# A projection of fourteen weight blocks by seven products for each pair of blocks

## The reference

```python
h = rmsnorm(x, norm_mix)                                  # 1056 x 1024
proj = h @ w_in                                           # columns q k v z | gates | u v' | c
qkv, new_conv = causal_short_conv(q|k|v, conv_buf, gdn_conv_w)   # 4 taps along tokens, then silu
q, k = l2norm(q), l2norm(k)
o = gated_delta_chunked(q, k, v, g, beta, state)          # o_a
u = gelu(ub); vs = layernorm(gelu(vb)); o_b = u * sgu_mix(vs)
pm = pc + rwkv_mu * (p_prev - pc)                         # then the rwkv7 recurrence, o_c
x = x + concat(o_a, o_b, o_c) @ w_out
x = x + hier_moe(rmsnorm(x, norm_ffn))                    # 16 experts, 2 for each token
y = rmsnorm(x, norm_final)
```

## Time and profile before

| | us |
|---|---|
| median of 3 runs | 1278.34 (1277.28 to 1280.43) |
| the profiled execution | 1276.18 |
| its span | 1274.4 |
| TensorE busy | 1208.9 (95%) |
| VectorE, ScalarE, GpSimd busy | 462.0, 348.8, 523.5 |

### The profile page before, as it was taken

The page is one execution under the profiler, slowest core; times in us unless marked ns, Lnnn a source line. Parts: engine busy times, 40 slices in busy tenths (PEclk is TensorE's granted clock), DMA queues, the critical chain, the costliest instruction groups (busy, mean ns, idle before and its releaser), DMA issues. The chain is left out here.

```text
span 1274.4 us, 31076 instructions
## 1 busy us (share of the span) xinstructions
PE 1208.9 (95%) x12624; PEld 825.0 (65%) x12624; DVE 462.0 (36%) x1140; ACT 348.8 (27%) x821; POOL 523.5 (41%) x790
## 2 busy tenths in 40 slices
PE   9999999999999999999998999959999999999990
PEld 7666666666656668877864554446777777777760
DVE  3135543345375624455441213252222222222223
ACT  4003112533342135555532232211111111111114
POOL 7100000020470036878833021026666666666662
PEclk9999999999999998999999999969999999999995
DMA  6111111125313100010075313279999897999838
GB/s 207 34 34 35 34 33 34 33 50 176 67 33 87 56 17 14 18 23 14 14 228 173 101 67 99 58 278 378 330 373 334 264 371 253 283 371 295 264 50 288
DMA packets 139879, 187.09 MB, mean 147 GB/s; under 512 B 37272, under 2 KB 85903, under 8 KB 139786
## 3 DMA queue, kind: packets, MB, share of 16 engines
q1 hardware_dynamic: 123018, 164.87, 38.3%
q0 software_dynamic: 15936, 20.57, 7.7%
q10 hardware_dynamic: 832, 0.33, 0.1%
HBM read 156.41 MB, written 29.32 MB: 146 GB/s over the span
## 5 line engine op out<-in xcount | busy, mean ns | idle before, releaser
L452 PE MATMUL ps<-hT,w_in 128*128 128x352 f32 (+1 forms) x1296 | 390.7, 461 | 1.8 <-ACT cb L690 1.2
L452 PEld LDWEIGHTS ps<-hT,w_in 128*128 128x128 f32 x1296 | 244.3, 190 | 138.4 <-issue 4.4
L2849 POOL DMA_INDIRECT sum_rows<-slot_out,scatter_rows x76 | 121.6, 1600 | 38.7 <-POOL scatter_rows L2848 25.4
L2894 PE MATMUL ps<-qkv,slot_T 128*32 128x256 f32 x1920 | 109.9, 379 | 2.1 <-DVE slot_T L2981 1.1
L2981 DVE TENSOR_TENSOR slot_T<-slot_raw_T,vecs 128x256 f32<-128x256 f32 x75 | 32.4, 433 | 208.5 <-PE ps L2894 207.6
L2894 PEld LDWEIGHTS ps<-qkv,slot_T 128*32 128x32 f32 x1920 | 74.4, 110 | 31.6 <-DVE slot_T L2981 3.2
L2826 POOL DMA_INDIRECT gathered<-h_rows,gather_rows x79 | 83.4, 1056 | 19.6 <-issue 12.2
L2938 ACT ACTIVATE slot_silu<-ps 128x128 f32<-128x128 f32 x77 | 21.5, 279 | 224.2 <-PE ps L2894 222.0
L2894 PE MATMUL ps<-cb,slot_T 128*32 128x256 f32 x1408 | 80.6, 379 | 0.0
L2894 PEld LDWEIGHTS ps<-cb,slot_T 128*32 128x32 f32 x1408 | 55.2, 110 | 20.8
L2944 ACT ACTIVATE slot_out<-ps,slot_weights 128x256 f32<-128x256 f32 x76 | 36.1, 475 | 112.1 <-PE ps L2905 112.1
(11 more groups left out here) (685 smaller groups left out, 1991.7 us busy)
## 6 DMA issues: line engine op xcount, KB each, us to landing
w_in<-in_w_in SPq DMA_DIRECT2D x28, 512.0 KB, 4.0
qkv<-in_expert_w_gate SPq DMA_DIRECT2D x6, 2048.0 KB
qkv<-in_expert_w_up SPq DMA_DIRECT2D x6, 2048.0 KB
qkv<-in_expert_w_down SPq DMA_DIRECT2D x6, 2048.0 KB
cb<-in_expert_w_gate SPq DMA_DIRECT2D x5, 2048.0 KB
cb<-in_expert_w_up SPq DMA_DIRECT2D x5, 2048.0 KB
zg<-in_expert_w_down SPq DMA_DIRECT2D x5, 2048.0 KB
third_w_down<-in_expert_w_down SPq DMA_DIRECT2D x5, 2048.0 KB
```

The costliest lines, as they stand in the source:

```text
L452: last = pe.matmul(pbank(b)[:, c, 0:n], w[:, k, :], hT[:, k, c * CH:c * CH + n], start=(k == 0), stop=(k == KD - 1))
L2849: pool.indirect_dma_start(quarter_sums, bass.IndirectOffsetOnAxis(ap=sidx[:, r:r + 1], axis=0), y[r][:], None, compute_op=ALU.add).then_in ...
L2894: last = pe.matmul(gu_bank[c4[c], 0:2 * QF].rearrange("p (x b d) -> p x b d", x=2, d=32), xT[:, k, :], of_quarter(by_block[u][k], c), star ...
```

## The change

The 14 blocks u0, u1, q0 to q11 become seven pairs. For a pair, the input (tokens in two halves of 528, channels in two halves of 512) and the weights (channels in two halves, two blocks of columns) are two by two blocks, and the product is made by seven products of half size in place of eight, by Winograd's form of Strassen's scheme. A chunk is 264 tokens of each token half; a pair has two chunks, `seven_products(p, 0)` and `(p, 1)`, of seven products with four matmuls each.

- VectorE makes the sums of the input once (S1 to S4, four operations of 128x2112) when `hT` is complete.
- GpSimd makes the four differences of the weights of each pair (`weight_sums`, 128x512 each). Those of pair 2 stand behind the wait for `shc` and two output transfers.
- The products rotate over six PSUM banks. A product waits until the one six before it has been read: by ScalarE for the first product M1 (`copied`), by VectorE otherwise (`half_add`).
- ScalarE copies only M1 to the destination; VectorE adds the other six products, with seven additions (`halves`), in place.
- The convolution reads the block from its place in `qkv`, with the last tap first, over 1056 tokens.
- On ScalarE, silu of pair p-1 stands behind the copies of pair p, and both `squares` now stand behind the last pair: squares(0) after silu 9, squares(1) after silu 10.
- The buffers for the spread norms of the two halves swap places, and several small buffers move.

The core of the diff (the destinations of buffers, index functions and renamed semaphores are left out):

```diff
+                def load_pair(p):
+                    for u in range(2):
+                        sp.wait_ge(w_in[u], 16 * (p + 1))
+                        load_w(2 + 2 * p + u, w_pair[p][u])
+                sp.wait_ge(s.xT, TILES)
+                load_pair(0)
+                load_pair(1)
+                sp.wait_ge(s.pj, at["v1"] + 1)
+                load_pair(2)
+                for p in range(3, 5):
+                    sp.wait_ge(s.prod, product(p - 2, 1, "M3"))
+                    load_pair(p)
+                sp.wait_ge(s.vout, 3)
+                sp.wait_ge(s.rows_out, 16)
+                load_pair(5)
+                load_pair(6)
...
             def _(pool):
...
+                def weight_sums(p):
+                    (wa, wb), (t1, t2, t3, t4) = w_pair[p], t_pair[p % 2]
+                    b11, b21, b12, b22 = (w[:, a:a + KH, :] for w in (wa, wb) for a in (0, KH))
+                    for u in range(2):
+                        pool.wait_ge(w_in[u], 16 * (p + 2))
+                    if p >= 2:
+                        pool.wait_ge(s.prod, product(p - 2, 1, "M3"))
+                    pool.tensor_tensor(t1, b12, b11, ALU.subtract)
+                    pool.drain()
+                    pool.tensor_tensor(t2, b22, t1, ALU.subtract)
+                    pool.tensor_tensor(t3, b22, b12, ALU.subtract)
+                    pool.drain()
+                    pool.tensor_tensor(t4, b21, t2, ALU.subtract).then_inc(s.sums_w, 1)
+                weight_sums(0)
+                weight_sums(1)
                 pool.wait_ge(s.samp_w, 16 * NB * H)
...
                 pool.wait_ge(s.shc, 2)
                 pool.dma_start(O["shift_prompt"]...
                 pool.dma_start(O["shift_sample"]...
+                weight_sums(2)
+                weight_sums(3)
                 pool.wait_ge(s.vn, 3)
...
+                for p in range(4, 7):
+                    weight_sums(p)
...
+                def seven_products(p, ch):
...
+                    def multiply(name, w, a):
+                        n = product(p, ch, name)
+                        chunk_of, back = divmod(n - 7, 7)
+                        if n <= 6:
+                            pe.wait_ge(s.ev, 1 + (n - 1) // 3)
+                        elif back == 0:
+                            pe.wait_ge(s.copied, chunk_of + 1)
+                        else:
+                            pe.wait_ge(s.half_add, 6 * chunk_of + back)
+                        for k in range(KH):
+                            last = pe.matmul(of_product(p, ch, name), w[:, k, :], a[:, k, x], start=k == 0, stop=k == KH - 1)
+                        last.then_inc(s.prod, 1)
+                    if ch == 0:
+                        for u in range(2):
+                            pe.wait_ge(w_in[u], 16 * (p + 2))
+                        pe.wait_ge(s.sums_w, p + 1)
+                    multiply("M1", b11, A11)
+                    multiply("M6", t2, S2)
+                    multiply("M2", b21, A12)
+                    multiply("M7", t3, S3)
+                    multiply("M4", t4, A22)
+                    multiply("M5", t1, S1)
+                    multiply("M3", b22, S4)
...
-                columns("u0")
+                seven_products(0, 0)
                 values(0)
-                columns("u1")
+                seven_products(0, 1)
                 values(1)
-                columns("q0")
+                seven_products(1, 0)
                 values(2)
+                seven_products(1, 1)
                 last_tokens(1)
...
+                seven_products(2, 0)
+                seven_products(2, 1)
+                mix(0)
+                seven_products(3, 0)
+                mix(1)
+                seven_products(3, 1)
+                mix(2)
+                seven_products(4, 0)
+                gate_columns()
+                seven_products(4, 1)
+                gate_transposes()
+                seven_products(5, 0)
+                seven_products(5, 1)
+                log_decay_sums()
+                seven_products(6, 0)
+                log_decay_rows()
+                seven_products(6, 1)
...
             # ScalarE, from pair 2 on (of_pair: wait for conv, silu)
+                pair_out(2)                      # copy(2,0) silu0 copy(2,1) silu1
+                pair_out(3)
+                copy(4, 0)
+                of_pair(3, 0)
...
+                copy(6, 0)
+                act.wait_ge(s.gate_dve, GATE_DVE["decays"])
...
+                of_pair(5, 0)
+                act.wait_ge(s.gate_pe, GATE_PE["rows"])
...
+                copy(6, 1)
+                of_pair(5, 1)
+                squares(0)
+                of_pair(6, 0)
+                squares(1)
+                of_pair(6, 1)
...
             # VectorE
+                dve.tensor_tensor(S1, A21, A22, ALU.add)
+                dve.tensor_tensor(S3, A11, A21, ALU.subtract)
+                dve.drain()
+                dve.tensor_tensor(S2, S1, A11, ALU.subtract)
+                dve.drain()
+                dve.tensor_tensor(S4, A12, S2, ALU.subtract).then_inc(s.hT, 1)
...
+                FIRST, REST = ("M6", "M2"), ("M7", "M4", "M5", "M3")
...
+                halves(1, 1, *FIRST)
                 scale(0)
+                halves(1, 1, *REST)
+                last_tokens(1)
+                halves(2, 0, *FIRST)
+                halves(2, 0, *REST)
+                conv(0)
+                halves(2, 1, *FIRST)
                 scale(1)
                 scale(2)
+                halves(2, 1, *REST)
+                conv(1)
+                gate(0)
+                halves(3, 0, *FIRST)
+                halves(3, 0, *REST)
+                conv(2)
...
+                halves(6, 0, *REST)
                 conv(8)
+                halves(6, 1, *FIRST)
+                halves(6, 1, *REST)
                 conv(9)
                 conv(10)
                 conv(11)
```

More of the change, by code:

```diff
@@ L167, in make_masks @@
     g.drain()
-    g.nop().then_inc(s.masks, 1)
+    g.nop().then_inc(s.consts, 1)
 def build(nc, A, O, debug=None):
@@ L256, in build @@
         at = {b: n for n, b in enumerate(order)}
-        weighted = [b for b in order if b[0] in "vuqcz"]
+        weighted = ["v0", "v1"] + [b for pair in pairs for b in pair] + [b for b in order if b[0] in "cz"]
         base = {"v": COL_U + DB, "u": COL_U, "q": 0, "c": COL_C, "z": 3 * DA}
@@ L578, in log_decay_rows @@
                     pe.transpose(ps[0:H, 7, 448:448 + NS], gcum[0:NS, NT, :], m.ident[0:NS, 0:NS]).then_inc(s.gate_pe, 1)
[L580 to L589, removed]
-                        gate_transposes()
+                seven_products(2, 0)
+                seven_products(2, 1)
+                pe.wait_ge(s.vc, 3)
+                pe.wait_ge(s.shc, 2)
+                mix(0)
[13 more added lines that the diff above has]
+                seven_products(6, 1)
                 def before_c(b, c):
+                    if (b, c) == ("c2", 0):
+                        pe.wait_ge(s.half_add, added(6, 1, "M3"))
                     for f in steps.get((b, c), ()):
@@ new lines, in _ @@
+                pair_out(0)
+                copy(1, 0)
+                of_pair(0, 0)
+                copy(1, 1)
+                act.wait_ge(s.var, 3)
+                act.activation(st4[:, 1], st4[:, 1], ACT.Ln, scale=1.0 / HC, bias=LN_EPS)
+                act.drain()
+                act.activation(st4[:, 1], st4[:, 1], ACT.Exp, scale=-0.5).then_inc(s.vr, 1)
+                of_pair(0, 1)
+                pair_out(2)
+                pair_out(3)
+                copy(4, 0)
+                of_pair(3, 0)
@@ new lines, in _ @@
+                act.wait_ge(s.gate_pe, GATE_PE["columns"])
+                act.activation(gt[:, 0:256], ps[:, 6, 0:256], ACT.Copy)
+                act.activation(gt[0:NS, 256:256 + NS], ps[0:NS, 6, 256:256 + NS], ACT.Copy).then_inc(s.gate_act, 1)
+                copy(4, 1)
+                of_pair(3, 1)
+                copy(5, 0)
+                act.wait_ge(s.gate_dve, GATE_DVE["inputs"])
+                act.activation(gtmp[:, 0], gtk[:, :, 0:H], ACT.Exp, scale=-1.0)
+                act.activation(gts[:, 0, :], gts[:, 0, :], ACT.Exp)
@@ new lines, in _ @@
+                act.activation(gtmp[:, 2], gtmp[:, 1], ACT.Abs)
+                act.drain()
+                act.activation(gtmp[:, 2], gtmp[:, 2], ACT.Exp, scale=-1.0)
+                act.drain()
+                act.activation(gtmp[:, 2], gtmp[:, 2], ACT.Ln, bias=1.0).then_inc(s.gate_act, 1)
+                of_pair(4, 0)
+                copy(5, 1)
+                of_pair(4, 1)
+                copy(6, 0)
+                act.wait_ge(s.gate_dve, GATE_DVE["decays"])
+                act.activation(kdf[:], kdf[:], ACT.Exp)
@@ L847, in _ @@
             def _(dve):
-                for u in range(2):
-                    dve.memset(pre[u][:, 0:3], 0.0)
                 dve.memset(st4[:], 1.0)
@@ L962, in conv @@
+                    a_s = acc[u][:, SEQ:NTOK].rearrange("p (b t) -> p b t", t=TB)
```

(5 more changed lines are left out.)

229 lines of the change are left out of this document (134 added, 95 removed).

## The result

The kernel after took 1289.18 us (median of 6 runs, 1284.07 to 1292.73), the one before 1277.67 on the same chips (6 runs, 1275.44 to 1280.43). The ratio is 1.0084, with a 95% interval of 1.006 to 1.0108: slower by 0.8%. The forecast was 1279.0 with a range of 1270 to 1287; the median lies 2.2 above the range.

What follows compares the result with a forecast made beforehand. TensorE, busy 95% of the span, was taken as the bound: -26.0 + 7.8 + 2.5 + 0.8 + 11.7 + 1.3 + 2.5 = +0.6 us on 1276.18, plus 2.16 to the median, gave 1279, range 1270 to 1287.

Steps and rivals of the forecast that it cites:

- the near grams: Small products behind c2, covered by the claim that everything from c2 on keeps its old relative schedule: no change.
- the prediction's own signs of being wrong: Either pause absent, a third over 2 us in pairs 3 to 6, passes over 230 ns apart, or changed length behind c2.
- the stretch behind c2: From c2 on, all was to run on the old relative schedule, moved as a whole.
- pause ahead of pair 2: TensorE waits for GpSimd's weight differences, behind the second last_tokens copy and two output transfers: 7.8 us, bounds 7.0 to 9.
- clock behind it: Behind each of the two long pauses TensorE's clock is low from its first pass: 2.5 us each.
- pair 3, chunk 0: TensorE waits before product M3 as GpSimd's pair 4 differences delay conv(1): 0.8 us, from 0 to 1.0, or 4.0.
- pause ahead of the norm products: Ahead of c2, TensorE waits for the first squares behind conv(9) and silu 9: 11.7 us plus 1.3 for the decays.
- the rival by which the pace is not reached: Each of 98 products loses 0.15 us to its wait and signal, 14.7 us in all: 1294, chance 0.08.
- the second rival: GpSimd holds VectorE up at conv(1) and conv(9), 6.5 us more than forecast: 1285.4, chance 0.18.
- the third rival's case: In the working on pair 3: by the skill's rule alone, conv(1) could be late by all 5.1 us.
- rival with pauses that cost only themselves: At the two long pauses, no clock lost (5.0 back) and no contention (2.1 back): 1271.8, faster, chance 0.23.

Runs made afterwards that it cites:

- transfers_last: Kernel after, with GpSimd's two output transfers moved behind the weight differences of pairs 2 and 3: 1288.64 us, ratio 1.009.
- sums2_early: Kernel after, with pair 2's weight differences moved ahead of GpSimd's wait for the copied rows and the two output transfers: 1277.09 us, ratio 1.0.
- decays_late: Kernel after, with GpSimd's first operation on the decays waiting until conv(9) is done: 1285.13 us, ratio 1.0064.
- squares_early: Kernel after, with squares(0) moved on ScalarE from behind silu 9 to ahead of silu 8: 1280.69 us, ratio 1.0035.
- after_again: Kernel after, measured once more unchanged: 1289.37 us, ratio 1.0097.
- pause_filled: Kernel after, with 40 matmuls of the identity, read by nobody, added ahead of pair 2: 1287.91 us, ratio 1.0077.
- before_padded: Kernel before, with 112 products of 32 columns, read by nobody, added at the start of TensorE's work: 1288.78 us, ratio 1.0086.
- all_moved_aligned: Kernel after with pair 2's differences, squares(0) and two logarithms early, pair 4's differences late, plus 8 products of 32 columns at the start: 1264.48 us, ratio 0.9894.
- sums4_late: Kernel after, with GpSimd beginning pair 4's differences only when conv(1) is done: 1288.47 us, ratio 1.0091.

## Why the prediction was wrong

The steps that failed are two waits and one stretch. The wait ahead of pair 2 was priced at 7.8, at most 9, and took 10.2, for a term put at nothing. The delay that GpSimd gives VectorE was priced too low at conv(1) and conv(9), so that pair 3 lost 2.8 in place of 0.8 and the norm products 14.0 in place of 13.0. And the near grams, put at no change, lost 2.2. Two of the prediction's own signs of being wrong came: a third pause of over 2 us (2.35, in pair 3) and another length of the stretch behind c2.

In the profiled executions the difference is 7.9 us where 0.6 was predicted. Term by term, from starts in the timeline:

| step | predicted | measured |
|---|---|---|
| the products | -26.0 | -25.6 (14 chunks of 12.46) |
| pause ahead of pair 2 | 7.8 | 10.2 |
| clock behind it | 2.5 | 2.3 |
| pair 3, chunk 0 | 0.8 | 2.8 |
| small gaps in the other chunks | 0 | 1.2 |
| pause ahead of the norm products | 13.0 | 14.0 |
| clock behind it | 2.5 | 1.4 |
| the near grams | 0 | 2.2 |

Before rounding the sum is 8.7; pair 0 had begun 0.4 earlier, and 0.4 came back behind the near grams.

- **The products** were right: 222.5 ns a pass against 222, taken between the rows of 256 and 352 columns. VectorE kept up, and the rival by which the pace is not reached did not come.
- **The pause ahead of pair 2** was in the right place with the right releaser; its size, and the upper bound of 9, failed. Missing was GpSimd's 2.49 us behind its own transfers: the prediction took 0.15 for each drain. transfers_last and sums2_early show that it belongs to the transfers. The trace of the kernel before had it to be read, as 3.07 us between the operations on the decays; with it in place of one drain the sum would have been 10.8, not 7.8.
- **Pair 3** was the second rival's mechanism and not the forecast's: conv(1) was late by 4.2, not by 1.9. I had taken conv(11) beside two decays as the price, when conv(1) meets four operations. The Trainium skill, "SBUF — State Buffer", section "Who interferes with whom", has the two engines hold the port in turn for a whole instruction; by that the delay is up to 5.1. The trace agrees, with 32 numbers in 1.26 us beside an operation of 1.26, and it was the better guide than the row. (The prediction's working calls this the third rival's case; in its list it is the second.)
- **The pause ahead of the norm products** was right but for conv(9), late by 2.4 in place of 1.3; decays_late took exactly that back. It also stood in the prediction that squares(0) had moved three blocks back in ScalarE's list; squares_early shows it as the cause.
- **The clock** was right for the first long pause (2.3 for 2.5). For the second it was 1.4 in this execution and 2.4 in after_again, so whether 2.5 was too dear depends on the execution. For the short pauses the cost was missing: behind 2.3 us the clock fell in some executions only. The rival with pauses that cost only themselves is refuted by the first eight passes of pair 2 and by pause_filled.
- **The stretch behind c2** was said to keep its distances. It lost 2.2 us to the gap in the near grams, of which the kernel before has none; before_padded and all_moved_aligned bring it in and take it out.

From 1284.07 to the median of 1289.18 it is 5.1 us, where the prediction carried over 2.2 from the kernel before. That the profiled execution was the fastest of six was luck. The comparison of two executions above puts 4.0 of their 7.3 us on the clock behind the pauses; the rest, and the single runs without a profile, stay open. So of the 10.2 us that the forecast was short, 7.3 are the terms above and some 3 this.

What each wait is worth in the median: sums2_early 12.3, squares_early 8.7, sums4_late 0.9 (a value that can't be told from nothing), together 21.9; all at once 25 to 26, with the logarithms moved as well.

## What to carry to other kernels

A cheaper product on the engine that bounds the kernel is worth what the lists of the other engines let through: here 25.6 of 26 us came, and two places in two lists took 27.9 with their clock. Before a transfer or a wait is put ahead of work that the bounding engine will want, look for work that could stand in front of it; moving one helper call ahead of a wait was worth 12 us. On a stretch without waits, price each new pause with its clock, and a pause of 2 us too. Before a cost is put at nothing, look for the same pair of instructions elsewhere in the trace: the drain behind a transfer was there, in another part of the list.

## What the runs showed of the hardware

- GpSimd stood still for 2.5 to 4.1 us at the first drain or operation that came behind transfers which it had issued itself (2.49, 2.78 and 3.90 in the kernel after, 3.33 in sums2_early, 4.06 in pause_filled), even 130 us after the transfer (3.07, in the kernel before). With drains in between it was 0.18 there, and none of four differences had such a gap when the two transfers stood behind them.
- An operation of VectorE on 32 numbers lasted 1.26 us in place of 0.25 beside one of GpSimd, and conv(1) 9.9 in place of 5.7.
- In bursts of short products TensorE stood still for 1.1 to 2.6 us, at places that moved with the number of rows ahead, modulo 128. With 16 rows more at the start of the program such a gap was gone 300 us later.
- Behind a pause of 2.3 us the clock fell to 0.50 in some executions and not in others, with the same kernel: 2.05 and 3.56 us for the same eight passes. Behind one of 0.61 us it did so too: 19.17 and 20.86 us for the same 64 passes, in kernels alike up to there.
- Products of 32 columns that go to four groups of partitions in turn came 9 ns apart, those to one group 33 to 35 ns.
